# A four-layer diffusion backbone on one core: RMS norms summed into columns and spread back by TensorE, half of the residual adds on GpSimd, filter tables loaded earlier

## The reference, cut to what matters

```python
def _rmsnorm(x, g):
    y = xf * lax.rsqrt(jnp.mean(xf * xf, axis=-1, keepdims=True) + EPS)
    return (y * g).astype(x.dtype)
...
    u_lat = _modulate(_rmsnorm(h_lat, g[0]), m_lat[0], m_lat[1])
    o_lat, o_ctx = _mixer(u_lat, u_ctx, ...)
    h_lat = h_lat + m_lat[2] * _rmsnorm(o_lat, g[1])
    f_lat = _conv_ffn(_modulate(_rmsnorm(h_lat, g[2]), m_lat[3], m_lat[4]), *ffn)
    h_lat = h_lat + m_lat[5] * _rmsnorm(f_lat, g[3])
    # the same for the context, except in the last layer
```

## Time and profile before

| what | value |
|---|---|
| time, median of 3 | 2417.85 us |
| time of the profiled execution | 2420.38 us |
| its span | 2418.5 us |
| PE busy | 2272.2 us, 94% of the span |
| DVE busy | 1594.0 us, 66% |
| ACT busy | 924.2 us, 38% |
| POOL busy | 269.1 us, 11% |
| mean granted TensorE clock | 0.971 of full speed |

### The profile page before, as it was taken

The page is one execution under the profiler, slowest core; times in us unless marked ns, Lnnn a source line. Parts: engine busy times, 40 slices in busy tenths (PEclk is TensorE's granted clock), DMA queues, the critical chain, the costliest instruction groups (busy, mean ns, idle before and its releaser), DMA issues.

```text
span 2418.5 us, 29957 instructions
## 1 busy us (share of the span) xinstructions
PE 2272.2 (94%) x11897; PEld 1843.6 (76%) x11897; DVE 1594.0 (66%) x2844; ACT 924.2 (38%) x1373; POOL 269.1 (11%) x273
## 2 busy tenths in 40 slices
PE   6999899999988988899999989998999999898998
PEld 4867688888866755688888867476888886767997
DVE  2425887777865533787777864868777776755554
ACT  3336443332243421443332243845333223455553
POOL 0000101010010015201010001120111000101111
PEclk8999999999998999999999999999999999999999
DMA  9450434445613210334445522031444453213553
GB/s 292 158 173 3 137 122 139 134 145 165 191 55 117 91 40 0 122 106 147 136 135 176 173 88 88 1 105 62 152 135 139 146 189 123 79 32 129 180 182 114
DMA packets 289904, 296.59 MB, mean 123 GB/s; under 512 B 6418, under 2 KB 288027, under 8 KB 289638
## 3 DMA queue, kind: packets, MB, share of 16 engines
q1 hardware_dynamic: 288125, 290.11, 37.3%
q0 software_dynamic: 1232, 4.42, 0.5%
q10 hardware_dynamic: 409, 0.16, 0.0%
HBM read 293.61 MB, written 1.05 MB: 122 GB/s over the span
## 4 chain that ended last, share of the span: by engine, by line
PE 83%; DVE 11%; ACT 2%; DMA 2%; issue 1%; POOL 1%; SPq 0%; ACTq 0%; POOLq 0%; DVEq 0%
PE lo L574 24%; PE lo L576 23%; PE lo L575 23%; PE modp L528 2%; DVE normed L1285 2%; PE lo L827 1%; DVE h L1290 1%; PE modp L542 1%; PE hi L840 1%; DVE conv L1282 1%; PE lo L727 1%; DVE probs L1393 1%; PE lo L747 1%; DVE probs L1419 1%; DVE normed L1315 1%
## 5 line engine op out<-in xcount | busy, mean ns | idle before, releaser
L574 PE MATMUL lo<-u_hi,w_hi 128*128 128x512 f32 (+1 forms) x2328 | 835.6, 359 | 24.0 <-DVE u_lo L1320 23.0
L575 PE MATMUL lo<-u_lo,w_hi 128*128 128x512 f32 (+1 forms) x2328 | 818.1, 351 | 0.0
L576 PE MATMUL lo<-u_hi,w_lo 128*128 128x512 f32 (+1 forms) x2328 | 817.9, 351 | 0.0
L1236 DVE TENSOR_TENSOR w_lo<-w_raw,w_hi 128x2048 fp32r<-128x2048 f32 (+2 forms) x182 | 407.7, 2240 | 349.5 <-ACT w_hi L928 349.5
L928 ACT ACTIVATE w_hi<-w_raw 128x2048 fp32r<-128x2048 f32 (+2 forms) x182 | 339.7, 1867 | 518.3 <-DMA w_raw<-in_ffn_w_down 257.3
L574 PEld LDWEIGHTS lo<-u_hi,w_hi 128*128 128x128 f32 x2328 | 445.7, 191 | 94.8 <-issue 34.5
L1252 DVE SCALAR_TENSOR_TENSOR mod_acc<-mod_raw,silu_c,mod_acc 128x256 f32<-128x256 f32 x1008 | 491.2, 561 | 0.1
L576 PEld LDWEIGHTS lo<-u_hi,w_lo 128*128 128x128 f32 x2328 | 445.6, 191 | 58.6
L575 PEld LDWEIGHTS lo<-u_lo,w_hi 128*128 128x128 f32 x2328 | 446.2, 192 | 56.3 <-issue 1.2
L574 PE MATMUL lo<-mid_hi,w_hi 128*128 128x512 f32 (+1 forms) x704 | 259.2, 368 | 0.2 <-DVE conv L1587 0.2
L576 PE MATMUL lo<-mid_hi,w_lo 128*128 128x512 f32 (+1 forms) x704 | 255.8, 363 | 0.0
(11 more groups left out here) (232 smaller groups left out, 2158.2 us busy)
## 6 DMA issues: line engine op xcount, KB each, us to landing
w_raw<-in_ffn_w_up SPq DMA_DIRECT2D x88, 1024.0 KB, 5.1
mod_raw<-in_mod_w SPq DMA_DIRECT2D x144, 512.0 KB, 3.7
w_raw<-in_ffn_w_down SPq DMA_DIRECT2D x32, 1024.0 KB, 5.2
mod_unit<-in_mod_w SPq DMA_DIRECT2D x24, 1024.0 KB, 6.7
w_raw<-in_a_w_qkv SPq DMA_DIRECT2D x12, 1024.0 KB, 5.2
w_raw<-in_ffn_w_down SPq DMA_DIRECT2D x16, 768.0 KB, 4.4
w_raw<-in_b_w_in SPq DMA_DIRECT2D x12, 1024.0 KB, 5.1
w_raw<-in_a_w_out SPq DMA_DIRECT2D x8, 1024.0 KB, 5.2
```

What stands on the lines that cost most here:

```text
L574: mm(o, h3[:, k, c], x, start=(first and k == 0), stop=False)
L575: mm(o, h3[:, k, c], y, start=False, stop=False)
L576: ins = mm(o, l3[:, k, c], x, start=False, stop=(last and k == nr - 1))
L1236: tt(WL[:, n % 3, 0:words], RAW[:, n % 3, 0:words], WH[:, n % 3, 0:words].bitcast(F32), ALU.subtract).then_inc(lo_ready, 1)
```

## The change

- Sums: each 128-column block of the squares becomes the weights, and one column of ones the moving operand. The sum over the partitions of 128 tokens then stands in one PSUM column (`sum_columns`). A chunk of 512 tokens takes 4 such matmuls, one of 256 tokens 2.
- The root and the reciprocal are taken on 2 or 4 columns. VectorE multiplies the identity with each column (`invert`, a 128x128 diagonal), and TensorE multiplies ones with the diagonals of a half (`spread`): the inverse root of each token stands in all rows of a PSUM bank, which VectorE reads from there.
- Residual: GpSimd adds the even chunks, VectorE the odd ones.
- `first_tiles` waits for the spread of the latent half, and does that of the context half inside its second tile.
- `load_filter` starts when layer 0's last tile is done, and one table has a place of its own.

```diff
             def first_tiles(n, q, sub, widths):
...
+                    if v == 0 and sub > 0:
+                        spread("h", sub, 0)
                     for t in ts:
+                            mid = v == 0 and V > 1 and sub > 0 and t == ts[-1]
                             tile(n + t, q + t, (v + 1) * SEQ, UH, UL, True, True, s0=v * SEQ,
+                                 after=(lambda k: spread("h", sub, 1) if k == 2 else None) if mid else None,
...
-            def sum_squares(s, out, first, last):
-
-                pe.wait_ge(sq_ready, s + 1)
-                mm(out, ones[:, :], SQ[:, s % 2, 0:out.shape[1]], start=first, stop=last).then_inc(stat_step, 1)
+            def sum_columns(src, at, nb, first, last):
+
+                for b in range(nb):
+                    ins = mm(bank[4][:, at + b:at + b + 1], src[:, b * P:(b + 1) * P], ones[:, 0:1],
+                             start=(first and b == 0), stop=(last and b == nb - 1))
+                ins.then_inc(stat_step, 1)
+
+            def spread(what, k, v):
+
+                pe.wait_ge(diag_ready, SPREAD[what, k, v] + 1)
+                mm(spread_bank(what, v), ones[:, :], diag(what, v), start=True, stop=True).then_inc(inv_spread, 1)
...
             def u_norm(k):
 
                 for v in range(UV[k]):
+                    pe.wait_ge(root_ready, ROOT["h", k, v])
                     for c in range(KT):
-                        sum_squares(SQH[k] + KT * v + c, bank[6 + v][:, 0:SEQ], c == 0, c == KT - 1)
+                        s = SQH[k] + KT * v + c
+                        pe.wait_ge(sq_ready, s + 1)
+                        sum_columns(SQ[:, s % 2, :], stat_cols("h", v), 2, c == 0, c == KT - 1)
...
             for r in range(8):
                 unit_rows(r)
                 unit_cols()
+            for v in range(2):
+                spread("h", 0, v)
...
+            def invert(what, k, vs):
+
+                dve.wait_ge(root_ready, ROOT["o", k] + 1 if what == "o" else ROOT["h", k, vs[-1]] + 1)
+                c0, c1 = stat_cols(what, vs[0]), stat_cols(what, vs[-1]) + 2
+                link(nc.vector.reciprocal(inv_rms[:, c0:c1], inv_rms[:, c0:c1]))
+                for v in vs:
+                    for b in range(2):
+                        at = stat_cols(what, v) + b
+                        ins = ts(diag(what, v)[:, b * P:(b + 1) * P], ident, inv_rms[:, at:at + 1], None, ALU.mult)
+                    ins.then_inc(diag_ready, 1)
...
                     for c in range(KT):
                         dve.wait_ge(o_ready, k * KT + c + 1)
-                        scaled(c)
-                        if c > 0:
+                        stt(TC[:, c, s], O[:, c, s], coef[:, v, 1 + 2 * (k % 2), c:c + 1], spread_bank("o", v), ALU.mult,
+                            ALU.mult).then_inc(gated, 1)
+                        if c % 2 == 0 and c > 0:
                             add(c - 1)
                     add(KT - 1)
...
+                        if c == 5 and v == 0 and UV[k] > 1 and k > 0:
+                            invert("h", k, [1])
...
+            def residual(k):
+
+                for v in range(OV[k]):
+                    s = slice(v * SEQ, (v + 1) * SEQ)
+                    for c in range(0, KT, 2):
+                        pool.wait_ge(gated, R0[k] + KT * v + c + 1)
+                        tt(H[:, c, s], H[:, c, s], TC[:, c, s], ALU.add).then_inc(h_even, 1)
...
             def load_filter():
 
-                pool.wait_ge(*u_part(2, 1, KT - 1))
+                pool.wait_ge(tile_done, FIRST["in", 1])
```

More of the change, by code:

```diff
@@ L393, in build @@
         SUMMED = {}
+        SPREAD = {}
         USED = []
@@ L406, in build, with h_part, stat_cols, spread_bank @@
             SUMMED["o", k] = nm
+            for v in range(OV[k]):
+                SPREAD["o", k, v] = len(SPREAD)
             ROOT["o", k], nr = nr, nr + 1
+        def h_part(k, v, c):
+            return h_odd if c % 2 else h_even, (R0[k] + KT * v) // 2 + c // 2 + 1
+        def stat_cols(what, v):
+            return 2 * v if what == "o" else 4 + 2 * v
+        def spread_bank(what, v):
+            return bank[6 + v if what == "o" else 7 - v][:, 0:SEQ]
+        def diag(what, v):
+            return (DIAG_O if what == "o" else DIAG_H)[:, v * SEQ:(v + 1) * SEQ]
         def u_part(k, v, c):
@@ L605, in o_norm @@
+            def spread(what, k, v):
+                pe.wait_ge(diag_ready, SPREAD[what, k, v] + 1)
+                mm(spread_bank(what, v), ones[:, :], diag(what, v), start=True, stop=True).then_inc(inv_spread, 1)
             def o_norm(k):
-                if k > 0:
-                    pe.wait_ge(root_ready, ROOT["o", k])
-                out = bank[4][:, 0:NL[k // 2]]
+                nb = NL[k // 2] // P
                 pe.wait_ge(sq_added, (k + 1) * (KT - 3))
-                mm(out, ones[:, :], SQA[:, 0:NL[k // 2]], start=True, stop=False).then_inc(stat_step, 1)
+                pe.wait_ge(root_ready, ROOT["o", k])
+                sum_columns(SQA, 0, nb, True, False)
@@ L612, in o_norm @@
                 for c in (KT - 2, KT - 1):
-                    sum_squares(SQO[k] + c, out, False, c == KT - 1)
+                    pe.wait_ge(sq_ready, SQO[k] + c + 1)
+                    sum_columns(SQ[:, c % 2, :], 0, nb, False, c == KT - 1)
+                for v in range(OV[k]):
+                    spread("o", k, v)
             def u_norm(k):
                 for v in range(UV[k]):
+                    pe.wait_ge(root_ready, ROOT["h", k, v])
                     for c in range(KT):
-                        sum_squares(SQH[k] + KT * v + c, bank[6 + v][:, 0:SEQ], c == 0, c == KT - 1)
+                        s = SQH[k] + KT * v + c
+                        pe.wait_ge(sq_ready, s + 1)
+                        sum_columns(SQ[:, s % 2, :], stat_cols("h", v), 2, c == 0, c == KT - 1)
@@ L773, in filter_stage @@
                         pe.wait_ge(mod_final, 3)
-                        mm(bank[6][0:FW, 0:SEQ], FWT[0:FEMB, 0:FW], FA[0:FEMB, 0, :], start=True, stop=True).then_inc(f_mm, 1)
+                        mm(bank[6][0:FW, 0:SEQ], FWT[0:FEMB, 0:FW], ZT[0:FEMB, :], start=True, stop=True).then_inc(f_mm, 1)
                     else:
@@ L940, in o_root @@
                 N = NL[k // 2]
-                root(SUMMED["o", k], bank[4][:, 0:N], RMS_O[:, 0:N])
+                root(SUMMED["o", k], bank[4][:, 0:N // P], inv_rms[:, 0:N // P])
             def norm_sums(k):
@@ L950, in norm_sums @@
                         elif v < OV[k - 1]:
-                            act.wait_ge(h_added, R0[k - 1] + KT * v + c + 1)
+                            act.wait_ge(*h_part(k - 1, v, c))
                         square(SQH[k] + KT * v + c, H[:, c, s], SEQ)
-                    root(SUMMED["h", k, v], bank[6 + v][:, 0:SEQ], RMS_H[:, s])
+                    at = stat_cols("h", v)
+                    root(SUMMED["h", k, v], bank[4][:, at:at + 2], inv_rms[:, at:at + 2])
             def unit_row(r):
@@ L1302, in pre_norm @@
                 if k > 0:
-                    dve.wait_ge(h_added, R0[k - 1] + KT * OV[k - 1])
-                else:
-                    for v in range(2):
-                        dve.wait_ge(root_ready, ROOT["h", k, v] + 1)
-                        link(nc.vector.reciprocal(RMS_H[:, v * SEQ:(v + 1) * SEQ], RMS_H[:, v * SEQ:(v + 1) * SEQ]))
+                    dve.wait_ge(h_even, (R0[k - 1] + KT * OV[k - 1]) // 2)
+                    dve.wait_ge(h_odd, (R0[k - 1] + KT * OV[k - 1]) // 2)
+                    invert("h", k, [0])
+                else:
+                    invert("h", 0, [0])
+                    invert("h", 0, [1])
                     lo(0)
@@ L1715, in _ @@
                 o_squares(2 * i)
+                residual(2 * i)
                 for c in range(FM):
@@ L1719, in _ @@
                 o_squares(2 * i + 1)
+                residual(2 * i + 1)
 def row_loads(a, rows):
```

27 lines of the change are left out of this document (13 added, 14 removed).

## The result

The changed kernel takes 2439.72 us (median of 4 runs, 2438.78 to 2439.95), the kernel before 2418.86 us beside it (4 runs, 2417.57 to 2421.93). The ratio is 1.0084, with a 95% interval from 1.0066 to 1.0101: slower by about 21 us. The profiled span is 2437.0 us against 2418.5, +18.5. The mean granted clock of TensorE fell from 0.971 to 0.945.

What follows compares the result with a forecast made beforehand. TensorE, busy 94% of the span, was taken as the bound. Terms 12.3 + 9.3 + 1.7 − 1.1 + 2.6 + 5 + 8.5 − 8.7 gave +29.6 on 2417.85: 2447.5 us, range 2408 to 2464.

Steps and rivals of the forecast that it cites:

- Column sum of a chunk: Input norm's sums: 0.97 us per chunk at half clock; each boundary +4.1 us behind a mixer, +3.1 behind an MLP.
- Output norm and first product: Beginning of each boundary: first product at 279.5 to 280.0 us, before 279.84, so no change.
- VectorE's residual: Products and adds inside a boundary: 10.1 us instead of 13.6, bounds 9.3 and 15.1, gain hidden.
- Layer 3's second boundary: The boundary with one half: about half the extra of the others, +1.7 us.
- Restarts and context spreads: First tiles about 2 us more at half clock, seven times, +5 us; six context spreads inside tiles, +2.6 us.
- Start: Start of the kernel: sums +4 us, modulation blocks at half clock +3.8, a spread +0.7, together +8.5.
- Filter tables: Filter stage: the wait for tables goes, −7.7 us, and TensorE loses less to half clock behind it, −1.
- End: End of the kernel: no input norm, a shorter reciprocal and four adds fewer, −1.1 us.
- the likeliest case: Whole kernel: the forecast of half clock through all new sums, chance 0.60, own range given as 2432 to 2461 us.
- Rival 1: Boundaries and start: weight loads alone keep the clock up, 0.54 us per chunk, −32, 2386 us; chance 0.08.
- Rivals 2, 3 and 5: Boundary clock rises midway, 2404 us, 0.07; filter gains 0 to 3, 2454, 0.07; fast and slow boundaries mixed, 2418, 0.05.
- Rival 4: Half clock as forecast, but the start hidden by transfers and restarts free: 2434 us; chance 0.13.

Runs made afterwards that it cites:

- e8: Kernel before, with early filter tables and GpSimd's even residual adds, both norms' sums wide as before: 2422.62 us, ratio 1.0011.
- e2: Changed kernel with the sums of `h` as 256-column matmuls again, without spreads of `h`: 2391.41 us, ratio 0.989.
- e4: Changed kernel with all residual adds on VectorE, none on GpSimd: 2439.74 us, ratio 1.0087.
- e3: Changed kernel with wide sums for only the first input norm, at the start of the kernel: 2432.73 us, ratio 1.0059.
- e1: Kernel before with only the early load of the filter tables, one with its own place: 2413.14 us, ratio 0.9982.
- e5: e2 with all residual adds back on VectorE: 2399.93 us, ratio 0.9916.
- e7: Changed kernel with one unused 128x256 matmul ahead of each pair of column sums of `h` at the seven boundaries: 2526.94 us, ratio 1.0442.
- e9: e2 with unused 128x128 matmuls at the seven boundaries, 4 behind the output norm's last sum, 7 behind its spreads: 2391.71 us, ratio 0.9889.

## Why the prediction was right, and where it was off

The sign, the order of size and the mechanism (half clock through the sums, sums on TensorE as the path, half clock behind them) were right: +29.6 forecast, +18.5 on the span and +20.9 on the medians. The clock was at half from 284.3, 2.9 us behind the start of the first sum, to about 311, TensorE's sums stood behind one another, VectorE waited 7.7 us for the last spread, and no wait for the tables is left. Step by step:

- **Column sum of a chunk, the mis-sized term.** Forecast 0.97 us at half clock, from four pairs with two moving columns and 0.03 for a wait; measured 0.85 from one to the next (a block of 8 spans 6.96), and no wait between: below the 0.9 to 1.0 that were to show it. Sixteen chunks a boundary: −1.9 us. The added 0.4 for the output norm did not come: first sum to first sum of `h` is 7.02 us (288.46 − 281.44), before 7.10. Together the mixer boundaries came out at +2.14, +1.47 and +1.48 and not +4.1, those behind an MLP at +1.0 and not +3.1. Boundaries: 23.3 forecast, 11.5 measured. This is as much as the whole miss of 11.1; the errors of the other terms nearly cancel.
- **Output norm and first product: nothing.** Right: the first product starts 5.14 us behind the first sum, before 5.38.
- **VectorE's residual.** Forecast 10.1 with bounds 9.3 and 15.1; measured 9.3, the bound without a lock. e8 shows the lock with the scale in SBUF, e2 none with it in PSUM. VectorE's gain was hidden here, as forecast (e4).
- **Layer 3's second boundary.** +1.7 forecast, +3.3 measured. 1.9 of it is no norm: ScalarE's squares come 3.78 us behind the first sum and not 1.89, behind a conversion that waited for its weight transfer (to 2210.58); 1.4 is the norm's share.
- **Restarts and context spreads.** Forecast 7.6 for seven restarts and six spreads, of which five and five, 5.7, lie in the five stretches. These show +1.25, +2.36, +2.54, +1.98 and +2.59, together 10.7: undersized by 5. The forecast took 2 us more at half clock at each restart. At two of the seven, behind the mixers of layers 1 and 2, the kernel before restarts at full clock, so that the whole 4 to 5 us there are new. In the five stretches together the changed kernel spends 16.7 us more at half clock. At the price that the kernel before shows (382.8 against 381.6 us for 3.4 us at half) that is about 6 us, an estimate; waits are 1.1, and the rest is left for the spreads. e2, without spreads and mostly at full clock, is 12.7 us shorter there than the changed kernel.
- **Start.** +8.5 forecast; +7.0 to the first boundary, of it +2.0 until the first block, +3.7 in the blocks, +0.6 to the first tile and +0.7 in the tiles. The sums were again the part that I had too high (+4): the first block, 4.95 us, still ran at full clock. e3 confirms the term by undoing it. The start of the kernel before is no fixed number, however: 270.0 to 274.5 us in before, e1 and e8, which have the same code there, so +7.0 could as well have been +11.
- **Filter tables.** −8.7 forecast, −8.2 measured, −7.3 in e1, whose total fell by 0.18% (some 4 us) in the medians. **End:** −1.1 and −2.5.
- **A slip in the range.** The lower end of the likeliest case, +17, gives 2435 and not 2432 us. The measured time lies above both.

Rival 1 (weight loads keep the clock up) is refuted for these sums by the 14.8 us window at 0.50 with TensorE occupied for 14.0. Rivals 2, 3 and 5 didn't come. Rival 4's time, 2434, lies nearer than it should by its reasons: neither the start nor the restarts were free.

What the experiments add is where the change's good half went. Early tables, columns for the output norm and GpSimd's adds are together worth 1.1% (e2); the columns for `h`, with their spreads, cost almost twice that, 48 us (2437.0 − 2388.8), as half clock in their own sums, at the start and in the tiles behind. No gain of GpSimd's share is shown by itself (e5). The prediction had seen the slack in VectorE but not that leaving `h` wide would turn it into time. One thing stays open: the prediction's reason for the half clock was that the sums move so little. e7, with wide matmuls in between, was at half clock too, so which part of the pattern keeps a fallen clock down is not shown, only that back-to-back wide sums bring it up and these sums do not.

## What to carry to other kernels

A statistic whose cost was hidden beside another engine can be made cheaper in work and dearer in time, because the wide matmuls that it removes also brought TensorE's clock back up: price what stands behind the removed work at half clock too. Here it paid to shorten the sums where the engine behind them waits (output norm) and to leave wide those that precede the tiles. Adds on GpSimd slowed VectorE while all its inputs lay in SBUF (e8), and did it no harm with one in PSUM (e2); they shortened the boundaries in neither. Before you believe a gain of a few us, compare the time at half clock in the stretches that you did not change.

## What was not expected of the hardware

- Alternating 128x256 matmuls and one-column pairs, TensorE occupied for 30.7 of 35.4 us, leaves a clock that has fallen at 0.50 (e7); in e9 it was up again 3.4 us after it had fallen, behind matmuls back to back.
- Two VectorE products beside a GpSimd add take 1.34 us with both tensor inputs in SBUF and 0.87 with one in PSUM (e8, e2).
- Stretches of the same code differ by 1 to 5 us between kernels: the filter stretch took 290.8 to 295.5 us in kernels that all have the early tables. TensorE's idle time in it is 20.7 us in all of them, and the time at half clock goes from 17 us (e2, 290.8) to 27 (e9, 295.5). At the start it is the clock as well (e1); at the end TensorE's waits differ too, by 3 to 7 us. A difference of 5 us in such stretches should not be read as their edit's worth.
